# A decoder block with expert retrieval on one core: 24 instead of 16 tokens in rows, and the low parts of 22 weight tiles made beforehand

## The chip, the cores and the metric

The kernel runs on one NeuronCore of a Trainium2 chip. The metric is the device time of one execution in microseconds (us); the median of three runs is given. The engines are TensorE (PE; PEld is its weight load), VectorE (DVE), ScalarE (ACT), GpSimd (POOL) and SyncE (SP, which here only issues transfers). A name with q behind it (SPq, ACTq, POOLq) is an engine's instruction queue: issues of transfers, waits.

## The reference

One layer on x of 512 tokens by 1024 channels, in float32:

```
xn = rmsnorm(h, norm_mix_g)
h  = h + hybrid_mixer(xn, ...)      # gated short convolution + causal pooling, products with w_in,
                                    # w_conv_out, w_pool_out and w_out
xn = rmsnorm(h, norm_ffn_g)
h  = h + peer(xn, w_query, sub_keys, expert_u, expert_v)
return rmsnorm(h, norm_final_g)

def peer(...):                      # 8 heads, 128 x 128 = 16384 experts, 16 chosen per head
    q = xn @ w_query;  scores = q . sub_keys            # two halves of 128 keys per head
    v1, i1 = top_k(scores[0], 16);  v2, i2 = top_k(scores[1], 16)
    best, pos = top_k(v1[:, None] + v2[None, :], 16)
    e1 = i1[pos // 16];  e2 = i2[pos % 16];  experts = e1 * 128 + e2;  gates = softmax(best)
    a = gelu(xn . expert_u[experts]) * gates            # 128 experts per token
    return a @ expert_v[experts]
```

## The kernel before

Every matrix product is made of three float32r products (high x high, high x low, low x high) that sum in PSUM. A weight tile is 128 x 1024 float32 (512 KB). For each tile SP loads `w_raw`, ACT rounds it into `w_hi` (line 589), VectorE subtracts to get `w_lo` (L1157), and TensorE makes 8 blocks x 3 matmuls (`tile_product`, L922 to L924). There are four slots (`SLOTS`) for each; the loops run over groups of four tiles, b being the slot. Counting semaphores tie them: `hi_done`, `lo_done`, `job_done` (tiles whose products are done), `bank_free`. SP loads tile n when `lo_done` has passed tile n - 4; ACT rounds it when TensorE has done tile n - 4.

The stages in order: 32 tiles of `w_in` with convolution and pooling (`in_block`), 4 pool tiles, 32 gate tiles (sigmoids, `merged_hi`/`merged_lo`), 8 of `w_out`, 16 of `query` with the scores; then the experts.

The experts: tokens 0 to 127 (`GT`) are worked in rows: GpSimd gathers for each of their 128 pairs one row of `u_rows` per token (`gather`, L538, an indirect transfer of 128 rows of 4 KB into one of 4 `ROW_SLOTS`), and VectorE multiplies and sums (`dot`, L1522), later the same with `v` (`v_row`, L1711). The other 384 tokens (`DT`) are worked densely: U holds all 16384 experts in 128 tiles (`u_tile`, 32 steps of 4), ACT applies gelu (`gelu_tile`, L746) and stores the activation to `act_dram`, except for the last `KEPT_STEPS` steps, which stay in memory. Of the 384, the last `EXTRA` = 16 tokens are taken out of the dense U product, so that its columns are `DENSE`, 368 of them; their pairs are worked in rows too, in groups of 8 tokens by 16 (`lay_extra`, `turn_extra`, `dot_extra`), with their values carried into the gates (`extra_gates`, with three-part gates `masks_x`), and the activation there is one.

While TensorE runs `u_tile` steps 1 to 11 (`TOPK_STEPS` = 12), VectorE searches the top 16 (`search`, `decode`) with the splits of the tiles put between its parts, by hand (`splits`). `u_dots` puts the row dots in: one in every second search step, then lists (`DOTS_BEFORE`, `DOTS_ROUND`, `DOTS_PLAIN`). The first gathers wait for `experts_ready`. Steps 15 to 26 (`onehot_round`, 6 rounds of 2 steps) also build the dense gate matrix from one-hot masks made by VectorE (16 tokens a mask; L1082, two matmuls a token, three for `masks_x`), which ACT copies and stores to `g_dram`. After the U part the V part: 128 tiles, `mask_a` multiplies activation and gate, `v_tile` has 18 matmuls of 512 columns; VectorE works the rest of the u dots and all 128 v rows there.

In the first tiles the order is by hand as well: ACT rounds x blocks (`xg_hi`) in the order of their arrival, the two halves of weight tile 0 between them, and squares them for the norm.

Of the kernel before, what the change touches and what calls it, by code (L numbers as in the profile page):

```python
# [75 lines left out]
EXTRA = 16  # L76
SHARED = 8
EXTRA_GROUPS = EXTRA // SHARED
SPREAD = P // SHARED
# [3 lines left out]
ROW_SLOTS = 4  # L83

# [14 lines left out]
U_STEPS = KEYS // SLOTS  # L99
TOKENS_PER_GROUP = 4  # L100
# [7 lines left out]
DOTS_TOPK = 1  # L108
# [3 lines left out]
ROWS_V = (DOTS_TOPK * (TOPK_STEPS // 2 - 1) + sum(DOTS_BEFORE) + ROUNDS * sum(DOTS_ROUND)  # L112
          + (U_STEPS - 1 - PLAIN_AT) * sum(DOTS_PLAIN))
# [5 lines left out]
assert U_STEPS - KEPT_STEPS >= PLAIN_AT and KEPT_STEPS == 5  # L119
# [100 lines left out]
def build(nc, x_t, params_d, w_in_d, pool_d, gate_d, w_out_d, query_d, keys_d, u_d, v_d, u_rows, gain_d, out_d,  # L220
          act_dram, g_dram, index_dram, extra_dram):
    ctx = ExitStack()
    with ctx:
# [11 lines left out]
        scratch = fixed("scratch", [P, 2, T])  # L235
        row_stat = fixed("row_stat", [P, T])
# [27 lines left out]
        norm_sq = in_loop("norm_sq", [P, T])  # L264
        gate_loop = MemoryMap(nc, front.at)
# [38 lines left out]
        expert_last = small("expert_last", [P, PAIRS], U32)  # L304
# [3 lines left out]
        gate_x = small("gate_x", [P, EXTRA_PARTS, EXTRA], BF16)  # L308
        assert small.at <= nc.sbuf_usable_end and small.at >= max(rest.at, after_topk.at)
        beside_xn = MemoryMap(nc, xn_at)  # L310
        x_extra = [beside_xn(f"x_extra{h}", [P, NB, T])[:, :, 0:GT] for h in range(EXTRA_GROUPS)]
# [4 lines left out]
        in_scratch = MemoryMap(nc, scratch_at)  # L316
        e1_b = in_scratch("e1_b", [P, DT], F16)
        e2_b = in_scratch("e2_b", [P, DT], F16)
        gate_b = in_scratch("gate_b", [P, GATE_PARTS, DT], F16)
        assert in_scratch.at <= scratch_at + 4 * 2 * T  # L320

        masks = [region(f"masks{k}", [P, 1 + GATE_PARTS, MASKED // 2, KEYS, 2], F16)
                 for k, region in enumerate((g_build, MemoryMap(nc, masks_at)))]
        masks_x = MemoryMap(nc, masks_at)("masks_x", [P, 1 + EXTRA_PARTS, MASKED // 2, KEYS, 2], BF16)
# [15 lines left out]
        def kept_at(k, b):  # L340

            if k == 0:
                return act_in[:, b, :]
            if k == 1:
# [3 lines left out]
            if k < KEPT_STEPS - 1:  # L348
                return kept[:, k - 2, b, :]
# [1462 lines left out]
```

## Time and profile before

| | us |
|---|---|
| median of three runs | 1618.13 (1618.07 to 1619.25) |
| the profiled execution | 1618.06 |
| its span, first to last instruction | 1616.2 |
| TensorE busy | 1607.6 (99%) |
| VectorE busy | 1281.6 (79%) |
| ACT busy | 690.6 (43%) |
| GpSimd busy | 370.1 (23%) |

The profile is of one execution. Busy time is the time in which an engine ran at least one instruction; a line's duration is from an instruction's start to its end, and as matmuls overlap in TensorE's pipeline, durations are longer than the distance from one start to the next. The granted TensorE clock was 1.0 throughout, the higher of its two levels (2.4 GHz). GpSimd does nothing from 3.6 us until 548 us.

### The profile page before, as it was taken

To read this page: it belongs to the slowest core of one execution; us is meant where nothing else is said; L and a number is where in the kernel's file an instruction comes from. 1 tells how busy PE (TensorE), PEld (TensorE's weight loads), DVE (VectorE), ACT (ScalarE), POOL (GpSimd) and SP (SyncE) were. 2 spreads that over 40 slices of the span, in tenths; PEclk is the share of its full clock that TensorE was granted. 3 is DMA by queue.
4 is the path that set the end of the run, shared out by engine and by line. 5 is a ranking of instruction groups with operands and counts; after the bars stand their busy time and mean duration, and the time that the engine had idled before them with its cause. 6 is when DMAs were issued, how large, how long until landed. Compare 5 with 4: busy or idle time off the path is not lost.

```text
span 1616.2 us, 25174 instructions
## 1 busy us (share of the span) xinstructions
PE 1607.6 (99%) x8581; PEld 1422.9 (88%) x8581; DVE 1281.6 (79%) x2311; ACT 690.6 (43%) x921; POOL 370.1 (23%) x286
## 2 busy tenths in 40 slices
PE   9999999999999999999999999999999999999998
PEld 7888888888888999999999999998888888888887
DVE  6855733335457999998999998778898999998997
ACT  5323423333325433334666766433334333333333
POOL 0000000000000100003222222433453445554551
PEclk9999999999999999999999999999999999999999
DMA  4322332222321655658899999998999999999994
GB/s 170 131 93 97 116 109 91 94 100 94 115 81 64 224 185 194 212 191 334 318 367 364 377 359 374 403 376 324 387 413 367 402 414 398 403 415 393 414 378 161
DMA packets 126919, 424.34 MB, mean 263 GB/s; under 512 B 16384, under 2 KB 19472, under 8 KB 125200
## 3 DMA queue, kind: packets, MB, share of 16 engines
q1 hardware_dynamic: 75168, 232.85, 39.3%
q0 software_dynamic: 39264, 142.64, 23.0%
q10 hardware_dynamic: 12432, 48.26, 7.6%
q8 instruction: 18, 0.29, 0.1%
q14 instruction: 37, 0.30, 0.0%
HBM read 375.18 MB, written 48.51 MB: 262 GB/s over the span
## 4 chain that ended last, share of the span: by engine, by line
PE 99%; DMA 0%; DVE 0%; ACT 0%; SPq 0%; issue 0%; ACTq 0%
PE bank L922 21%; PE bank L923 20%; PE bank L924 20%; PE bank L1104 11%; PE bank L1106 11%; PE bank L1105 11%; PE bank L1082 3%; PE bank L988 1%; DMA w_raw<-w_in 0%; PE bank L968 0%; PE bank L967 0%; PE bank L969 0%; PE bank L1118 0%; DVE u_lo L1203 0%; PE bank L1039 0%; PE bank L940 0%
## 5 line engine op out<-in xcount | busy, mean ns | idle before, releaser
L1157 DVE TENSOR_TENSOR w_lo<-w_raw,w_hi 128x1024 fp32r<-128x1024 f32 x347 | 423.4, 1220 | 147.3 <-ACT w_hi L589 142.3
L589 ACT ACTIVATE w_hi<-w_raw 128x1024 fp32r<-128x1024 f32 x347 | 366.3, 1057 | 353.2 <-PE bank L1106 214.9
L922 PE MATMUL bank<-xn_hi,w_hi 128*128 128x368 f32 (+1 forms) x1472 | 516.6, 351 | 0.1
L924 PE MATMUL bank<-xn_hi,w_lo 128*128 128x368 f32 (+1 forms) x1472 | 510.7, 347 | 0.0
L923 PE MATMUL bank<-xn_lo,w_hi 128*128 128x368 f32 (+1 forms) x1472 | 510.6, 347 | 0.0
L538 POOL DMA_INDIRECT rows<-u_rows,expert x128 | 156.0, 1218 | 958.5 <-DVE expert L1558 544.4
L1104 PE MATMUL bank<-w_hi,a_hi 128*128 128x512 f32 x768 | 298.9, 389 | 0.0
L1106 PE MATMUL bank<-w_hi,a_lo 128*128 128x512 f32 x768 | 298.8, 389 | 0.0
L1105 PE MATMUL bank<-w_lo,a_hi 128*128 128x512 f32 x768 | 298.8, 389 | 0.0
L922 PEld LDWEIGHTS bank<-xn_hi,w_hi 128*128 128x128 f32 x1472 | 276.2, 188 | 17.8 <-issue 0.6
L924 PEld LDWEIGHTS bank<-xn_hi,w_lo 128*128 128x128 f32 x1472 | 276.1, 188 | 17.6
L923 PEld LDWEIGHTS bank<-xn_lo,w_hi 128*128 128x128 f32 x1472 | 276.4, 188 | 17.2 <-issue 0.2
L538 POOL DMA_INDIRECT rows<-v,expert x128 | 189.3, 1479 | 189.5 <-DVE out_tok L1711 172.8
L1106 PEld LDWEIGHTS bank<-w_hi,a_lo 128*128 128x128 f32 x768 | 144.1, 188 | 30.1
L1105 PEld LDWEIGHTS bank<-w_lo,a_hi 128*128 128x128 f32 x768 | 144.2, 188 | 29.9
L1104 PEld LDWEIGHTS bank<-w_hi,a_hi 128*128 128x128 f32 x768 | 144.1, 188 | 29.8
L1711 DVE SCALAR_TENSOR_TENSOR out_tok<-rows,dots,out_tok 128x1024 f32<-128x1024 f32 x128 | 163.8, 1280 | 8.0 <-DMA rows<-v,expert 4.6
L1522 DVE SCALAR_TENSOR_TENSOR rows<-rows,x_tok 128x1024 f32<-128x1024 f32 x128 | 154.7, 1218 | 18.2 <-DMA rows<-u_rows,expert 18.1
L746 ACT ACTIVATE act_out<-bank 128x368 f32<-128x368 f32 x112 | 53.6, 479 | 219.9 <-PE bank L924 209.8
L848 ACT ACTIVATE a_hi<-a_f 128x384 fp32r<-128x384 f32 x128 | 67.0, 523 | 99.6 <-DVE a_f L1692 96.9
L760 ACT ACTIVATE g_sb<-bank 128x512 f32<-128x512 f32 x96 | 101.3, 1172 | 4.8 <-PE bank L1082 4.8
L1698 DVE TENSOR_TENSOR a_lo<-a_f,a_hi 128x384 fp32r<-128x384 f32 x128 | 70.4, 550 | 0.0
(225 smaller groups left out, 1381.7 us busy)
## 6 DMA issues: line engine op xcount, KB each, us to landing
w_raw<-u SPq DMA_DIRECT2D x128, 512.0 KB
w_raw<-v SPq DMA_DIRECT2D x128, 512.0 KB
g_dram<-g_sb ACTq DMA_DIRECT2D x12, 2048.0 KB, 10.6
g_in<-g_dram SPq DMA_DIRECT2D x84, 256.0 KB
act_dram<-act_out ACTq DMA_DIRECT2D x54, 384.0 KB
act_in<-act_dram SPq DMA_DIRECT2D x54, 384.0 KB
w_raw<-gate SPq DMA_DIRECT2D x32, 512.0 KB
w_raw<-w_in SPq DMA_DIRECT2D x31, 512.0 KB
```

The lines of the kernel that those rows point to most:

```text
L538: pool.indirect_dma_start(out=rows[:, slot, :], out_offset=None, in_=table.rearrange("a p d -> (a p) d"), in_offset=bass.IndirectOffsetOnA ...
L589: act.activation(w_hi[:, slot, :], w_raw[:, slot, :], ACT.Copy).then_inc(hi_done, 1)
L760: act.activation(g_sb[:, k, :, t:t + TOKENS_PER_GROUP].rearrange("p e t -> p t e"), bank[4 + q % SLOTS][:].rearrange("p (t e) -> p t e", e ...
L922: pe.matmul(out, hi, x_hi, start=k == 0, stop=False)
L923: pe.matmul(out, hi, x_lo, start=False, stop=False)
L924: last = pe.matmul(out, lo, x_hi, start=False, stop=k == NB - 1)
L1104: pe.matmul(out, a_h, v_hi, start=False, stop=False)
L1105: pe.matmul(out, a_h, v_lo, start=False, stop=False)
L1106: return pe.matmul(out, a_l, v_hi, start=False, stop=final)
L1157: dve.tensor_tensor(w_lo[:, slot, :], w_raw[:, slot, :], w_hi[:, slot, :].bitcast(F32), ALU.subtract).then_inc(lo_done, 1)
L1522: dve.scalar_tensor_tensor(rows[:, slot, :], rows[:, slot, :], 1.0, x_tok[:], ALU.mult, ALU.mult, accum_out=dots[:, ds(r)]).then_inc(rows_ ...
L1711: dve.scalar_tensor_tensor(out_tok[:], rows[:, slot, :], dots[:, ds(r)], out_tok[:], ALU.mult, ALU.add).then_inc(v_rows_used, 1)
```

## The change

- `EXTRA` goes from 16 to 24: three groups of 8 tokens, a third `x_extra` in the memory of `scratch`, the dense product of 360 columns. Three-part gates now hold for the last 32 tokens (`EXTRA_SPAN`), in two masks. `extra_t` is fetched in six transfers of four tokens, one before each of six `gelu_tile` calls, in place of one transfer.
- The number of u dots goes from 144 to 152. In the search steps 2 to 11 there are two in each (20) where there was one in every second (5); the V part has 37 instead of 44.
- 22 low parts, those of the odd slots (b = 1, 3) of U steps 2 to 12, are no longer made by VectorE. After tile 3 GpSimd loads each such tile (`low_raw`), multiplies it by -1 into float32r (`low_part`), adds the tile to it by an accumulating transfer, and stores the sum to `low_dram`, in two slots. ACT waits for all the stores ahead of the gate loop, as the slots lie where the gate loop has its tiles. In the retrieval GpSimd loads each low part straight into `w_lo` when the tile four before is done, in program order with its gathers, and TensorE waits for it. VectorE's next split counts two on `lo_done`.
- Six steps are kept instead of five; the first kept one lies in `x_extra`.
- At the start ACT and VectorE work the second half of weight tile 0 after x block 3 instead of after block 1, and the first two squares after weight tile 1.

The core of the diff:

```diff
-EXTRA = 16
+EXTRA = 24
 SHARED = 8
 EXTRA_GROUPS = EXTRA // SHARED
+EXTRA_LOAD = 4
+EXTRA_BANK = (6, 4, 6)
...
-DOTS_TOPK = 1
+DOTS_TOPK = 2
...
-EXTRA_FIRST = DOTS_TOPK * (TOPK_STEPS // 2 - 1) + sum(DOTS_BEFORE)
+EXTRA_FIRST = DOTS_TOPK * (TOPK_STEPS - 2) + sum(DOTS_BEFORE)
 EXTRA_END = EXTRA_FIRST + EXTRA
 EXTRA_SHOWN = EXTRA_FIRST - sum(DOTS_BEFORE) + ROW_SLOTS
-assert EXTRA_END <= EXTRA_FIRST + 2 * sum(DOTS_ROUND) and EXTRA == MASKED
-KEPT_STEPS = 5
...
+KEPT_STEPS = 6
+assert U_STEPS - KEPT_STEPS >= PLAIN_AT - ROUND and KEPT_STEPS == 6
+KEPT_J = DT // P
...
+def low_tile(k):
+
+    return SLOTS * (k // 2 + 2) + 2 * (k % 2) + 1
...
+        low_raw = in_loop("low_raw", [P, LOW_SLOTS, D])
+        low_part = in_loop("low_part", [P, LOW_SLOTS, D], F32R)
...
                     if b % 2 == 1 and g >= KEPT_STEPS:
 
-                        sp.wait_ge(af_ready, b + 1 if g == KEPT_STEPS else SLOTS * (g - 1) + b + 1)
+                        sp.wait_ge(af_ready, SLOTS * (1 if g == KEPT_STEPS else g - 1) + b + 1)
...
+            def load_low(k):
+
+                slot, times = k % LOW_SLOTS, k // LOW_SLOTS
+                if times > 0:
+                    pool.wait_ge(low_stored[slot], 16 * times)
+                pool.dma_start(low_raw[:, slot, :], u_d[low_tile(k)]).then_inc(low_raw_loaded[slot], 16)
+
+            def sum_low(k):
+
+                slot, times = k % LOW_SLOTS, k // LOW_SLOTS
+                pool.wait_ge(low_raw_loaded[slot], 16 * (times + 1))
+                pool.tensor_scalar(low_part[:, slot, :], low_raw[:, slot, :], -1.0, None, ALU.mult
+                                   ).then_inc(minus_high, 1)
+                pool.wait_ge(minus_high, k + 1)
+                pool.dma_start(low_part[:, slot, :], u_d[low_tile(k)], accum_op=ALU.add).then_inc(low_summed[slot], 16)
+
+            def store_low(k):
+
+                slot, times = k % LOW_SLOTS, k // LOW_SLOTS
+                pool.wait_ge(low_summed[slot], 16 * (times + 1))
+                pool.dma_start(low_dram[k], low_part[:, slot, :]).then_inc(low_stored[slot], 16)
+
+            pool.wait_ge(job_done, SLOTS)
+            for k in range(N_LOW + 2):
+                if k >= 2:
+                    store_low(k - 2)
+                if 1 <= k <= N_LOW:
+                    sum_low(k - 1)
+                if k < N_LOW:
+                    load_low(k)
...
+            def load_low_part(k):
+
+                pool.wait_ge(job_done, AT_U + low_tile(k) - SLOTS + 1)
+                pool.dma_start(w_lo[:, low_tile(k) % SLOTS, :], low_dram[k]).then_inc(low_loaded[k % 2], 16)
+
             for q in range(U_ROWS):
+                if q >= ROW_SLOTS and (q - ROW_SLOTS) % DOTS_TOPK == 0:
+                    step = (q - ROW_SLOTS) // DOTS_TOPK + 3
+                    for n in range(1, 4) if q == ROW_SLOTS else (step,) if step < TOPK_STEPS else ():
+                        load_low_part(2 * n - 2)
+                        load_low_part(2 * n - 1)
...
-                if j == 1:
+                if j == NB // 2 - 1:
                     act.wait_ge(raw_loaded[0], 16)
                     act.activation(w_hi[:, 0, HALF:], w_raw[:, 0, HALF:], ACT.Copy).then_inc(hi_done, 1)
-                    square_x(0)
-                    square_x(1)
             split_weight(1, 1, 1)
-            for j in range(2, NB):
+            for j in range(NB):
...
+            for k in range(LOW_SLOTS):
+                act.wait_ge(low_stored[k], 16 * len(range(k, N_LOW, LOW_SLOTS)))
             with act.Fori(0, NB) as i:
...
+            def load_extra(k):
+
+                tokens = slice(EXTRA_LOAD * k, EXTRA_LOAD * (k + 1))
+                act.dma_start(extra_t[:, tokens], extra_dram[tokens, :].rearrange("t p -> p t"),
+                              allow_slow_non_contiguous=True).then_inc(extra_loaded, 16)
+
             def g_round(s, last=False):
                 for b in range(ROUND * SLOTS):
+                    if isinstance(s, int) and s == ROUNDS - 2 and b < EXTRA // EXTRA_LOAD:
+                        load_extra(b)
...
+                if whole is not None:
+                    pe.wait_ge(hi_done, n + 1)
+                    pe.wait_ge(*whole)
+                elif halves:
...
+            def u_tile(step, b, parts=None, low=False):
+                tile_product(SLOTS * step + (AT_U + b), b, step + (USES_U + 1), xn_hi, xn_lo, parts, NB, tokens=DENSE,
+                             whole=(low_loaded[b // 2], 16 * step - 16) if low and b % 2 == 1 else None)
...
+                u_tile(1, b)
+            with pe.Fori(2, TOPK_STEPS + 1) as step:
+                for b in range(SLOTS):
+                    u_tile(step, b, low=True)
+            with pe.Fori(TOPK_STEPS + 1, ONEHOT_AT - 1) as step:
...
-                        if last_round and q >= GROUPS_PER_ROUND - SLOTS:
-                            held, parts = masks_x, EXTRA_PARTS
+                        if last_round and q // SLOTS >= EXTRA_MASK % MASKS_PER_ROUND:
+                            held, parts = masks_x[q // 4 % 2], EXTRA_PARTS
...
+            def split_weight(n, slot, tiles=1):
 
                 dve.wait_ge(hi_done, n + 1)
                 dve.tensor_tensor(w_lo[:, slot, :], w_raw[:, slot, :], w_hi[:, slot, :].bitcast(F32),
-                                  ALU.subtract).then_inc(lo_done, 1)
+                                  ALU.subtract).then_inc(lo_done, tiles)
...
+                from_memory = lambda group, b: 2 <= group <= TOPK_STEPS and b % 2 == 1
+                if not from_memory(step + 1, b):
+                    last = from_memory(step + 1, b - 1) if b > 0 else from_memory(step, SLOTS - 1)
+                    split_weight(SLOTS * step + (AT_U + SLOTS + b), b, 2 if last else 1)
...
-                    u_dots(rows_done, DOTS_TOPK)
-                    rows_done += DOTS_TOPK
                 else:
                     search(chunk, i, at, [a, b, c, none])
                     decode(chunk, 2 * (i - 1), at[0], d)
+                if n >= 2:
+                    u_dots(rows_done, DOTS_TOPK)
+                    rows_done += DOTS_TOPK
```

## Rows read from the trace of the kernel before

**Rows 1.** The profile's page, part 4: the chain that ended last, by engine.

```profile
PE 99%; DMA 0%; DVE 0%; ACT 0%; SPq 0%; issue 0%; ACTq 0%
```

**Rows 2.** Timeline of TensorE, first and last of 46 starts, then of 62.

```profile
119.66 0.39 PE L924 MATMUL bank<-xn_hi,w_lo 128*128 128x512 f32 x1
...
129.86 0.39 PE L924 MATMUL bank<-xn_hi,w_lo 128*128 128x512 f32 x1
...
699.79 0.33 PE L922 MATMUL bank<-xn_hi,w_hi 128*128 128x368 f32 x1
...
709.95 0.33 PE L923 MATMUL bank<-xn_lo,w_hi 128*128 128x368 f32 x1
```

**Rows 3.** Busy time by stretch of the span, columns named in the text below.

```profile
40.00:187.00 147.00, 147.00 (x651) 121.70 (x650) 98.11 (x138) 45.64 (x60) 0.00 (x0) 1.00 0.31 106
...
546.00:755.00 209.00, 208.94 (x1254) 208.57 (x1253) 197.31 (x732) 77.91 (x110) 21.67 (x21) 1.00 0.65 221
755.00:1010.00 255.00, 255.00 (x2030) 248.22 (x2029) 237.34 (x270) 171.84 (x206) 70.60 (x58) 1.00 0.96 359
```

**Rows 4.** The chain that ended last in order of time: start us, length us, what.

```profile
755.45 0.98 PE bank L1061 x9
768.42 0.94 PE bank L1082 x16
...
997.67 1.39 PE bank L1082 x24
```

**Rows 5.** Timeline of the start, then the transfers issued in its first 20 us.

```profile
2.15 0.70 SPq L437 DMA_DIRECT2D h_t<-x_t  x1
...
10.90 2.55 ACT L604 ACTIVATE u_hi<-h_t,params 128x512 fp32r<-128x512 f32 x4
...
14.58 1.05 ACT L589 ACTIVATE w_hi<-w_raw 128x1024 fp32r<-128x1024 f32 x1
...
16.94 0.50 PE L922 MATMUL bank<-u_hi,w_hi 128*128 128x512 f32 x1
...
h_t<-x_t SPq DMA_DIRECT2D x1, 512.0 KB, 8.4
```

**Rows 6.** The page, part 5: groups of instructions, columns as the page names them.

```profile
L1157 DVE TENSOR_TENSOR w_lo<-w_raw,w_hi 128x1024 fp32r<-128x1024 f32 x347 | 423.4, 1220 | 147.3 <-ACT w_hi L589 142.3
...
L924 PEld LDWEIGHTS bank<-xn_hi,w_lo 128*128 128x128 f32 x1472 | 276.1, 188 | 17.6
...
L1522 DVE SCALAR_TENSOR_TENSOR rows<-rows,x_tok 128x1024 f32<-128x1024 f32 x128 | 154.7, 1218 | 18.2 <-DMA rows<-u_rows,expert 18.1
```

**Rows 7.** Timeline of TensorE at tile 4, of ACT before gate tile 4.

```profile
35.43 0.50 PE L922 MATMUL bank<-u_hi,w_hi 128*128 128x512 f32 x1
...
220.73 1.06 ACT L589 ACTIVATE w_hi<-w_raw 128x1024 fp32r<-128x1024 f32 x1 [4.38 <-PE bank L924]
```

**Rows 8.** Transfers with us to landing; groups of GpSimd's instructions.

```profile
out<-out_sb SPq DMA_DIRECT2D x7, 256.0 KB, 2.0
...
keys_t<-keys SPq DMA_DIRECT2D x1, 1024.0 KB, 5.5
...
index_dram<-expert_last POOLq DMA_DIRECT2D x1, 8.0 KB, 1.6
...
L553 POOL DMA_DIRECT2D expert_extra<-index_dram x2 | 1.2, 594 | 0.0
...
L533 POOL TENSOR_SCALAR_AFFINE_SELECT ident<-ident 128x128 f32<-128x128 f32 x1 | 0.3, 293 | 0.2 <-POOL iota_key L530 0.2
...
L525 POOL MEMSET z_pad<- 128x2 f32 x1 | 0.1, 96 | 0.0
```

**Rows 9.** Timeline of GpSimd and of ACT, then transfers from 546 to 570 us.

```profile
552.40 0.94 POOL L538 DMA_INDIRECT rows<-u_rows,expert  x1 [0.30 <-issue]
...
559.20 0.48 ACT L746 ACTIVATE act_out<-bank 128x368 f32<-128x368 f32 x1 [2.66 <-PE bank L924]
...
GB/s 273 0 0 0 266 379 106 232 369 321 314 328 239 341 382 389 335 259 253 300 294 376 411 410 415 403 246 41 20 164 321 348 343 343 10 0 0 0 0 0
```

More of the change, by code:

```diff
@@ L83 @@
 ROW_SLOTS = 4
+LOW_SLOTS = 2
 TOP_A, LOW_B = 4, 4
@@ L99 @@
 U_STEPS = KEYS // SLOTS
+N_LOW = 2 * (TOPK_STEPS - 1)
 TOKENS_PER_GROUP = 4
@@ L235, in build @@
         scratch = fixed("scratch", [P, 2, T])
+        row_stat_at = fixed.at
         row_stat = fixed("row_stat", [P, T])
@@ L307, in build @@
         extra_t = small("extra_t", [P, EXTRA])
-        gate_x = small("gate_x", [P, EXTRA_PARTS, EXTRA], BF16)
+        gate_x = small("gate_x", [P, EXTRA_PARTS, EXTRA_SPAN], BF16)
         assert small.at <= nc.sbuf_usable_end and small.at >= max(rest.at, after_topk.at)
         beside_xn = MemoryMap(nc, xn_at)
-        x_extra = [beside_xn(f"x_extra{h}", [P, NB, T])[:, :, 0:GT] for h in range(EXTRA_GROUPS)]
+        x_extra = [beside_xn(f"x_extra{h}", [P, NB, T])[:, :, 0:GT] for h in range(2)]
+        x_extra.append(MemoryMap(nc, scratch_at)("x_extra2", [P, NB, GT])[:])
         assert beside_xn.at <= scratch_at
@@ L366, in sem @@
             return ctx.enter_context(nc.semaphore(name))
+        low_raw_loaded = [sem(f"low_raw_loaded{k}") for k in range(LOW_SLOTS)]
+        minus_high = sem("minus_high")
+        low_summed = [sem(f"low_summed{k}") for k in range(LOW_SLOTS)]
+        low_stored = [sem(f"low_stored{k}") for k in range(LOW_SLOTS)]
+        low_loaded = [sem(f"low_loaded{k}") for k in range(SLOTS // 2)]
         x_loaded = [sem(f"x_loaded{k}") for k in range(X_PARTS)]
@@ L742, in gelu_tile @@
                     to = kept_at(step - (U_STEPS - KEPT_STEPS), b)
-                if not stored and step < U_STEPS - 1:
-                    act.activation(to[:, DU:], ones[:, 0:EXTRA], ACT.Copy).then_inc(ones_set, 1)
-                    act.wait_ge(ones_set, SLOTS * (step - (U_STEPS - KEPT_STEPS)) + b + 2)
-                act.activation(to[:, 0:DU], bank[b][:, DENSE], ACT.Gelu).then_inc(act_ready, 1)
+                if not stored and step == U_STEPS - KEPT_STEPS:
+                    whole = KEPT_J - 1
+                    act.activation(to[:, whole, DU - whole * P:], ones[:, 0:EXTRA], ACT.Copy).then_inc(ones_set, 1)
+                    act.activation(to[:, 0:whole, :], bank[b][:, GT:GT + whole * P].rearrange("p (j t) -> p j t", t=P),
+                                   ACT.Gelu).then_inc(ones_set, 1)
+                    act.wait_ge(ones_set, 2 * b + 3)
+                    act.activation(to[:, whole, 0:DU - whole * P], bank[b][:, GT + whole * P:T - EXTRA], ACT.Gelu
+                                   ).then_inc(act_ready, 1)
+                else:
+                    if not stored and step < U_STEPS - 1:
+                        act.activation(to[:, DU:], ones[:, 0:EXTRA], ACT.Copy).then_inc(ones_set, 1)
+                        act.wait_ge(ones_set, SLOTS * (step - (U_STEPS - KEPT_STEPS) + 1) + b + 2)
+                    act.activation(to[:, 0:DU], bank[b][:, DENSE], ACT.Gelu).then_inc(act_ready, 1)
                 split_weight(SLOTS * step + (AT_U + SLOTS + b), b, step + (AT_U // SLOTS + 2))
@@ L1047, in _ @@
                         pe.wait_ge(scores_ready, HALVES)
+                    elif b == 1:
+                        pe.wait_ge(x_tok_ready, 2)
                     else:
-                        pe.wait_ge(x_tok_ready, 2)
+                        pe.wait_ge(x_extra_ready, 2)
                     turn_extra(b)
-            with pe.Fori(1, ONEHOT_AT - 1) as step:
+            for b in range(SLOTS):
+                u_tile(1, b)
+            with pe.Fori(2, TOPK_STEPS + 1) as step:
+                for b in range(SLOTS):
+                    u_tile(step, b, low=True)
+            with pe.Fori(TOPK_STEPS + 1, ONEHOT_AT - 1) as step:
                 for b in range(SLOTS):
@@ L1212, in _ @@
                                       ALU.subtract).then_inc(lo_done, 1)
-                    dve.wait_ge(squared, 2)
-                    chain.did(dve.tensor_tensor(squares[:, 0, :], squares[:, 0, :], squares[:, 1, :], ALU.add))
             split_weight(1, 1)
-            for j in range(2, NB):
+            for j in range(1, NB):
                 dve.wait_ge(squared, j + 1)
-                chain.wait()
+                if j > 1:
+                    chain.wait()
                 add = dve.tensor_tensor(squares[:, 0, :], squares[:, 0, :], squares[:, j, :], ALU.add)
```

81 lines of the change are left out of this document (45 added, 36 removed).

## The prediction, made before the change was run

> **What bounds the kernel.** First the page: of the span of 1616.2 us the chain that ended last is 99% TensorE [rows 1]. So the time is the sum of TensorE's own work plus the gaps in it, and an edit counts only if it shortens a matmul, adds one, or makes TensorE wait. Next I ask whether a matmul's cost follows its columns. The PE timeline shows 46 starts of 512-column matmuls from 119.66 to 129.86 us, one every 10.20/45 = 0.2267 us, and 62 starts of 368-column ones from 699.79 to 709.95 us, one every 10.16/61 = 0.1666 us [rows 2]. (The duration printed, 0.33 or 0.39, holds the pipeline's depth and is no spacing.) The slope is 60.1 ns over 144 columns, 0.417 ns a column, and 13 ns are fixed. Last, the stages: how near VectorE and the transfers are to full where the change gives them work [rows 3]. Columns there: length, then busy us of PE, PEld, DVE, ACT, POOL, clock, DMA share, GB/s. VectorE is 67% busy in the input products, 94% in the retrieval (546 to 755 us), 93% in the one-hot rounds (755 to 1010 us), where the DMA share is 0.96. TensorE is full in all three.
>
> **The change part by part.**
> *24 tokens in rows.* The dense products of the retrieval run over 360 columns instead of 368: 128 tiles x 8 blocks x 3 products = 3072 matmuls, 8 x 0.417 = 3.34 ns each: -10.26 us. A tile of 24 products falls from 4.00 to 3.92 us.
> The third group of 8 tokens costs eight more transposes; nine took 0.98 us [rows 4], so +0.87 us. The gates come in three parts for the last 32 tokens instead of the last 16: 16 more 128-column matmuls. 16 took 0.94 us and 24 took 1.39 [rows 4]: 0.45 per eight, +0.90 us.
> *The start.* ACT now converts x blocks 2 and 3 before the second half of weight tile 0, and all squares after weight tile 1. Before, ACT came to block 2 only at 10.90 us; tile 1's weights were converted at 14.58 and its products began at 16.94 us [rows 5]. The x part issued on SP at 2.15 us lands 8.4 us later, at 10.6 us [rows 5]: now blocks 2 and 3 are done before it, blocks 4 to 7 take 2.6 us from 10.6, the weights 1.05 us more (14.3 us), their low part on VectorE 1.22: tile 1 begins at 15.6 us, 1.35 earlier. Tile 2 then waits for the squares' sum and its low part and begins some 1.05 us earlier. I take -1.05 us; bounds 0 and -1.6.
> *VectorE.* In the retrieval it loses 22 splits of 1.22 us (26.8) and gains 15 dots of 1.22 (18.3) [rows 6]: from 197 to 189 us in a stage that shrinks from 209 to 205. In the one-hot rounds its work stays (one mask part more, 1.2 us), and the stage gets 3 us shorter: 237.3 of 255 becomes 238.5 of 252, 95%. Behind the retrieval products it has 7 dots less. All this is off the path as long as it stays under 100%: no cost. Cover gone, a step costs the difference.
> *Kept step, loads in pieces.* Four activations fewer to store and to fetch, six small transfers in place of one; ACT is idle half the time. No cost.
> *Making the 22 low parts.* A chain on GpSimd: load the tile, negate it (rounded), add the tile by an accumulating transfer, store; two slots. ACT waits for all stores before the gate products, since the slots' memory becomes merged_lo and the sigmoids. It begins when tile 3 is done, 35.43 - 1.05 = 34.4 us [rows 7]. Behind ACT's wait stand sig_a, the next w_hi (1.05) and VectorE's w_lo (1.22), and TensorE needs these for gate tile 4 at 220.73 - 1.05 = 219.7 us [rows 7]; so the stores must be in by 219.7 - 0.60 - 1.05 - 1.22 = 216.8 us. No row has such a transfer, so I bound it. 256 KB landed in 2.0 us and 1 MB in 5.5 (stages with free transfers), so 512 KB of data are worth 2.33; 8 KB from GpSimd landed in 1.6 us [rows 8]: load and store 3.9 us each. The adding transfer: no less than 3.9; if the data part doubles because two sources are read, 6.2, and if everything doubles, 7.8. It moves three streams where a copy moves two, so I take 3.9 + 1.2 = 5.1. Issue on GpSimd: 0.6. Negation of 1024 elements: from 2 elements 0.096 us and 128 elements 0.293 [rows 8], 1.56 ns an element: 1.6 us. With two slots and GpSimd in program order a tile takes the larger of half the round, (3.9 + 1.6 + 5.1 + 3.9)/2 = 7.3, and 5.1 + 0.6 + 1.6 = 7.3 us. End: 34.4 + (3.9 + 1.6 + 5.1 + 3.9) + 21 x 7.3 = 202 us, 15 us in hand: no cost. It decides at 8.0 us a tile, that is an adding transfer of 5.8 us. Transfers there: 106 GB/s at a share of 0.31 now, plus 1.57 MB every 7.3 us = 215 GB/s: 321, below the 359 of the one-hot rounds.
> VectorE and GpSimd: VectorE is busy 98 of 147 us there [rows 3]. The Trainium skill ("SBUF — State Buffer", "Who interferes with whom") says that a VectorE instruction with two inputs in SBUF and a GpSimd one that reads SBUF lock each other out for a whole instruction. Nothing in this trace runs arithmetic on GpSimd beside VectorE, so no run here shows it yet; what it would do is the first rival.
> *Loading them.* Two loads a step. Each is issued when the tile four before is done and needed three tiles (11.8 us) later, against 0.6 + 3.9 us plus contention (the stage goes from 221 to some 315 GB/s with 22 loads and 15 gathers more): hidden, but for the first. Behind such a load's wait on GpSimd's queue stand the two gathers of that step, whose dots come a step later: hidden. The count of low parts done now moves for an odd tile with the even one behind it, so SP's reload of an odd slot waits one split longer (4 us of some 12 that it has), and behind it the next load. The third group's transposes wait for the copies of the first, made a tile before. The first four gathers, the last of them issued at 552.40 us, fill the transfers (300 to 415 GB/s) until 561.6 us (the GB/s line has 40 slices of 0.6 us from 546 us) [rows 9]. The low part of tile 9 is queued behind them on the same queue. Its 0.52 MB at 400 GB/s end at 562.9 us and land at some 563.2, less the 1.05 won at the start: 562.2 us. Tile 9's products began at 559.1 us (ACT took tile 8's result at 559.20) [rows 9], now at 559.1 - 1.05 + 0.87 - 9 x 0.08 = 558.2 us. TensorE waits +4.0 us, once; bounds 0 (if the gathers are through sooner) and 6 (if w_raw's stream takes half of the 400, and landing takes another us). Behind the wait every later product is queued; ACT and VectorE only get ahead.
>
> **Sum**, against the profiled run's own 1618.06 us (span 1616.2; the median is 1618.13, so nothing to convert): -10.26 - 1.05 + 0.87 + 0.90 + 4.0 = -5.5, thus 1612.5 us.
>
> **Rivals.**
> (a) *The chain of low parts is late*, the one that ends slower. Condition: over 8.0 us a tile. If each negation waits for one VectorE instruction of 1.22 us, a tile takes 8.5 and the end is 34.4 + 15.7 + 178.5 = 228.6 us, 11.8 late, TensorE idle before gate tile 4: 1624.3 us. If the adding transfer takes 7.8 us, a tile takes 10.0, the end is 262 and the time 1657. For it: the margin is 7% a tile, and two of its terms are in no row. Against: negation and copies are taken high, since the queues there are two thirds empty.
> (b) *No wait at tile 9*: the transfers reach 415 GB/s in single slices, and w_raw can be put off; 1608.5 us.
> (c) *The one-hot rounds do not get faster.* VectorE at 95% and transfers at 0.96 leave 12 us and little else; if one is the bound, the 70 tiles from 755 us on keep their 0.08 us each: 1612.5 + 5.6 = 1618.1. Against: VectorE's idle time is spread over every round.
> (d) *The columns do not count any more*: PEld is busy 208.6 of 209 us in the retrieval [rows 3], a load 188 ns [rows 6] where a matmul starts every 167. If the load were the floor, the 10.26 are lost: 1622.8. Against: at the 2.4 GHz granted (clock 1.00 in every row) 512 columns are 213.3 ns and 368 are 153.3, and both spacings lie 13.3 ns above that, so the columns set the pace at both; a floor would have to lie in the 3.3 ns below.
>
> **Chances.** Forecast 0.43; (a) 0.31, of which 0.02 late by under 2 us, 0.08 by 2 to 9, 0.21 by more; (b) 0.12; (c) 0.09; (d) 0.05. 0.2% is 3.2 us, about what a measurement of this kernel can tell from no change, so the borders are 1614.9 and 1621.4. Faster: 0.43 + 0.12 + 0.02 = 0.57; same: 0.09 + 0.08 = 0.17; slower: 0.21 + 0.05 = 0.26. The range goes from a us under (b) to (a)'s first price, 1607.5 to 1624.5, and leaves out only the late half of (a). The forecast's own is 1609 to 1615.
>
> **What would show it.** Spacing of the 360-column matmuls 163.3 ns (d: 166.6). Tile 1 at 15.6 us. GpSimd's last store before 217 us and no idle TensorE before gate tile 4 (a: idle there, ACT's sig_a released by a store). One wait of TensorE near 558 us, some 4 us, released by the transfer of a low part, and no others at later odd tiles. VectorE under 97% between 750 and 1005 us. I am wrong if the accumulating transfer is far from a copy, or if loads in the retrieval land later than 11 us.

## The result and the profile after

The changed kernel takes 1684.18 us (median of four runs, 1681.18 to 1687.09), the kernel before 1618.69 us on the same chip: a ratio of 1.0404 (95% interval 1.0390 to 1.0417). It is 4% slower, not 0.35% faster as forecast. The profiled execution has 1681.18 us and a span of 1679.4, 63.2 us more than before. The page shows at once where to look. First the slices of the span, then the chain that ended last, both from the changed kernel's page:

```profile
PE   9999921999999999999999999999999999999998
...
PEclk9999965999999999999999999999999999999999
```

```profile
PE 73%; DMA 11%; DVE 8%; POOL 4%; issue 2%; ACT 1%; SPq 0%; DVEq 0%; ACTq 0%; POOLq 0%
```

TensorE is empty in one place, a seventh of the way in, and the chain that was 99% TensorE [rows 1] now holds transfers and GpSimd. The list of waits (engine, tile and line, what it waited for: us in total, times, longest us) names the place, and the timeline of TensorE shows it:

```profile
ACT L741 <- DMA low_dram<-low_part: 82.0, 1, 82.0
...
PE bank L1007 <- DVE w_lo L1250: 67.8, 3, 66.8
PE bank L1007 <- DMA w_lo<-low_dram: 2.5, 1, 2.5
```

```profile
219.13 0.39 PE L1009 MATMUL bank<-mix_hi,w_lo 128*128 128x512 f32 x1
...
286.29 0.79 PE L1007 MATMUL bank<-xn_hi,w_hi 128*128 128x512 f32 x1 [66.77 <-DVE w_lo L1250]
...
291.57 0.47 PE L1007 MATMUL bank<-xn_hi,w_hi 128*128 128x512 f32 x1
```

The releaser printed is VectorE's split, but that took 1.2 us. Behind it stands ACT, which waited 82.0 us for the last store of a low part (the 22nd), with the activations for gate tile 4 in its queue. This is rival (a)'s place and its signature, at nearly six times its first price (66.8 us for 11.8). Why the last store came so late is read from the chain that ended last, in order of time (start us, length us, what), one of its rounds and the end:

```profile
220.10 2.78 POOL low_part L573
222.88 0.29 issue
223.17 0.60 POOL low_part L576
223.77 6.02 DMA low_raw<-u
...
273.30 5.27 DMA low_part<-u
278.57 0.29 issue
278.86 2.98 DMA low_dram<-low_part
```

A round is negation 2.8, a pause of 0.3, issue of the adding transfer 0.6, then the landing of the next tile's load, 6.0 us here: some 10 us. Over all 22 it is 11.0 us a tile ((270.2 - 39.8)/21, from the first line below; median, shortest and longest of a negation are in it as 2772, 2767 and 3084 ns). The transfers' medians from issue to landing follow it, 512 KB each:

```profile
L573 POOL TENSOR_SCALAR low_part<-low_raw x22: 2767/2772/3084, 39.8 to 270.2; 128x1024 fp32r<-128x1024 f32 x22
...
low_raw<-u POOLq DMA_DIRECT2D x22, 512.0 KB, 6.9
low_part<-u POOLq DMA_DIRECT2D x22, 512.0 KB, 5.4
low_dram<-low_part POOLq DMA_DIRECT2D x22, 512.0 KB, 3.5
w_lo<-low_dram POOLq DMA_DIRECT2D x22, 512.0 KB, 5.6
```

By stretch (columns as for [rows 3]): the first answers to its first row, then the idle stretch, then its other two.

```profile
40.00:187.00 147.00, 147.00 (x650) 121.78 (x649) 101.05 (x138) 45.69 (x60) 62.71 (x52) 1.00 0.81 239
...
220.00:286.00 66.00, 0.00 (x0) 0.00 (x0) 1.07 (x1) 3.93 (x5) 28.37 (x23) 0.53 0.52 141
...
546.00:755.00 209.00, 206.53 (x1248) 199.92 (x1247) 187.31 (x796) 86.98 (x125) 31.03 (x36) 1.00 0.69 236
755.00:1010.00 255.00, 254.16 (x1911) 248.95 (x1911) 242.26 (x374) 156.05 (x194) 76.64 (x66) 1.00 0.95 357
```

The last two stretches are shifted against the kernel's stages by the 67 us. Over the idle stretch the granted clock is 0.53 in the mean, so for nearly all of it TensorE has the lower of its two levels (1.2 GHz), and it comes back at that level: the 12 matmuls from 286.29 to 291.57 start 0.44 us apart instead of 0.227, 2.6 us lost.

**Columns.** The TensorE timeline, first and last of 62 starts of 360-column matmuls, in two places (the first answers to the second pair of [rows 2]):

```profile
605.72 0.33 PE L1008 MATMUL bank<-xn_lo,w_hi 128*128 128x360 f32 x1
...
615.75 0.33 PE L1009 MATMUL bank<-xn_hi,w_lo 128*128 128x360 f32 x1
...
699.29 0.32 PE L1008 MATMUL bank<-xn_lo,w_hi 128*128 128x360 f32 x1
...
709.05 0.32 PE L1009 MATMUL bank<-xn_hi,w_lo 128*128 128x360 f32 x1
```

10.03/61 = 164.4 ns, and 9.76/61 = 160.0 ns: two spacings of one matmul, neither the 163.3 forecast. The shorter one holds from tile 9's wait at 627.6 us to another wait at 764.7, for 839 of the 3072.

**The balance** of the span, after less before: +66.8 (idle before gate tile 4), +2.6 (clock behind it), +2.6 (one wait at tile 9, starts at 627.59 and 630.39), +1.0 (a wait at 764.7), -1.3 (start: tile 4 begins at 34.14 us, 35.43 before [rows 7]), +1.8 (transposes and masks), and the columns 839 x 6.7 ns + 2233 x 2.2 ns = -10.5: +63.0 of 63.2.

### The profile page after: what moved, and what is told of

Its sections match the earlier page's. It is cut to its first block, busy times and chain, and to the rows that moved or that the text cites. A ratio compares the mean times of both kernels' runs of the same rounds, so it can differ in the third digit from the quotient of the medians.

```text
span 1679.4 us, 25386 instructions
## 1 busy us (share of the span) xinstructions
PE 1601.5 (95%) x8605; PEld 1415.5 (84%) x8605; DVE 1275.5 (76%) x2307; ACT 691.9 (41%) x932; POOL 489.9 (29%) x405
## 4 chain that ended last, share of the span: by engine, by line
PE 73%; DMA 11%; DVE 8%; POOL 4%; issue 2%; ACT 1%; SPq 0%; DVEq 0%; ACTq 0%; POOLq 0%
PE bank L1007 13%; PE bank L1008 13%; PE bank L1009 13%; PE bank L1198 10%; PE bank L1199 10%; PE bank L1197 10%; DMA low_raw<-u 9%; POOL low_part L573 4%; PE bank L1175 3%; DVE rows L1617 1%; DMA low_part<-u 1%; POOL low_part L576 1%; DVE less L1520 1%; DVE w_lo L1250 1%; DVE top_i L1519 1%
## 5 line engine op out<-in xcount | busy, mean ns | idle before, releaser
L1007 PE MATMUL bank<-xn_hi,w_hi 128*128 128x360 f32 (+1 forms) x1472 | 514.3, 349 | 70.1 <-DVE w_lo L1250 67.6
L1250 DVE TENSOR_TENSOR w_lo<-w_raw,w_hi 128x1024 fp32r<-128x1024 f32 x325 | 399.5, 1229 | 223.7 <-ACT w_hi L656 214.6
L1008 PE MATMUL bank<-xn_lo,w_hi 128*128 128x360 f32 (+1 forms) x1472 | 508.8, 346 | 0.0
L1009 PE MATMUL bank<-xn_hi,w_lo 128*128 128x360 f32 (+1 forms) x1472 | 508.3, 345 | 0.0
L595 POOL DMA_INDIRECT rows<-v,expert x128 | 178.2, 1392 | 217.1 <-DVE out_tok L1815 197.1
L822 ACT ACTIVATE act_out<-bank 128x360 f32<-128x360 f32 x108 | 51.0, 472 | 171.6 <-PE bank L1009 164.3
```

The source lines that it names most:

```text
L595: pool.indirect_dma_start(out=rows[:, slot, :], out_offset=None, in_=table.rearrange("a p d -> (a p) d"), in_offset=bass.IndirectOffsetOnA ...
L1007: pe.matmul(out, hi, x_hi, start=k == 0, stop=False)
L1008: pe.matmul(out, hi, x_lo, start=False, stop=False)
L1009: last = pe.matmul(out, lo, x_hi, start=False, stop=k == NB - 1)
L1250: dve.tensor_tensor(w_lo[:, slot, :], w_raw[:, slot, :], w_hi[:, slot, :].bitcast(F32), ALU.subtract).then_inc(lo_done, tiles)
```

## The experiments

Ten kernels. Eight undo, resize or reorder a part of the changed kernel, and two measure TensorE alone. Of each edit the lines that matter are shown.

**1. No low parts by GpSimd (no_low_chain).** 24 tokens in rows stay; VectorE makes all low parts, and the dots of the retrieval are as before.

```
-                from_memory = lambda group, b: 2 <= group <= TOPK_STEPS and b % 2 == 1
+                from_memory = lambda group, b: False
-            for k in range(N_LOW + 2):
+            for k in range(0):
-DOTS_TOPK = 2
+DOTS_TOPK = 1
```

> Changed kernel without the chain of low parts and with the row dots where they were before (one in every second search step); 24 tokens in rows, the sixth kept step and the new order of the start stay. Theory A (the loss of 65 us is the chain alone; the rest of the prediction's sum holds): 1618.1 - 10.3 - 1.3 + 0.9 + 0.9 = 1608.3 us, no idle TensorE after 16 us, matmuls of 360 columns 163.3 ns apart. Rival B (part of the loss, or of the gain, hangs on VectorE with 8 dots more in the V part, or on the one-hot rounds that cannot go faster): 1612 us or more, with waits of TensorE after 560 us.

Measured: 1616.66 us (ten runs), before 1618.40; ratio 0.9990 (0.9980 to 0.9999). The 67 us are gone, so they belong to the low parts. But the gain is not the forecast's (rival B: over 1612 us, with waits after 560). TensorE's waits, and its timeline close to V's end:

```profile
PE bank L1005 <- DVE w_lo L1248: 2.0, 3, 1.3
PE bank L1195 <- DVE a_lo L1800: 1.9, 1, 1.9
```

```profile
1592.96 0.39 PE L1197 MATMUL bank<-w_hi,a_lo 128*128 128x512 f32 x1
1595.25 0.47 PE L1195 MATMUL bank<-w_hi,a_hi 128*128 128x512 f32 x1 [1.90 <-DVE a_lo L1800]
...
1598.33 0.63 PE L1197 MATMUL bank<-w_hi,a_lo 128*128 128x512 f32 x1
1598.75 0.60 PE L1195 MATMUL bank<-w_hi,a_hi 128*128 128x512 f32 x1
```

A wait of 2 us there also brought TensorE to its lower level: starts 0.43 us apart until 1599. VectorE has eight more dots than before and no room for them behind the retrieval. So the low parts are not an extra: they pay for the rows.

**2. Four slots, negation in place (four_slots).** The load is issued two tiles ahead; all 22 low parts.

```
-LOW_SLOTS = 2
+LOW_SLOTS = 4
+        low_part = MemoryMap(nc, in_loop.at - 4 * LOW_SLOTS * D)("low_part", [P, LOW_SLOTS, D], F32R)
-            for k in range(N_LOW + 2):
-                if k >= 2:
-                    store_low(k - 2)
-                if 1 <= k <= N_LOW:
-                    sum_low(k - 1)
+            for k in range(N_LOW + 3):
+                if 2 <= k <= N_LOW + 1:
+                    sum_low(k - 2)
                 if k < N_LOW:
                     load_low(k)
+                if k >= 3:
+                    store_low(k - 3)
```

> Chain of 22 low parts with four slots, negated in place, each load issued two tiles before its negation. Theory A1 (a tile took 10.6 us because a load could be issued only behind the add of the tile before, and had to land, 6.9 us, before the next negation of 2.8): now the tile takes what GpSimd itself needs, 6 to 7 us, the last store lands near 195 us, no wait of ACT, 1611.8 us (1608.3 + 2.6 at tile 9 + 0.9 near 764 us). Rival A2 (the transfers of that stage are full, share 0.81, and each simply takes as long as the engines give): the tile stays at 9 us or more, the last store lands after 235 us, TensorE idles 20 us or more, 1630 us or more.

Measured: 1624.05 us, four runs from 1616.16 (the profiled one) to 1628.72; ratio 1.0042 (1.0026 to 1.0059). In the profiled run a tile takes 7.5 us, the last store releases ACT at 214.05, and TensorE has no gap ahead of the gates. GpSimd's negations, the stretch from 40 to 187 us, and ACT's timeline:

```profile
L573 POOL TENSOR_SCALAR low_part<-low_raw x22: 2797/2806/3192, 40.5 to 197.7; 128x1024 fp32r<-128x1024 f32 x22
```

```profile
40.00:187.00 147.00, 147.00 (x649) 121.36 (x648) 110.12 (x137) 45.43 (x59) 93.26 (x76) 1.00 1.00 297
```

```profile
214.05 1.28 ACT L741 ACT_TABLE_LOAD   x1 [13.63 <-DMA low_dram<-low_part]
```

The time lies between the two theories. The transfers are full, a share of 1.00 at 297 GB/s, so 7.5 us a tile is about what they allow here, only 0.5 us under the forecast's deciding 8.0. ACT's release at 214.05 comes 2.7 us before the forecast's 216.8, but the true deadline is earlier (see below) and leaves 1.2 us. That the other three runs are 8 to 13 us longer fits a chain that is sometimes that much later; this is not shown, as only the fastest of the four has a trace.

**3. Without the adding transfer (no_add).** The low parts are then only minus the high parts, so the result is not the reference's. The store waits for the negation alone.

```
-                pool.dma_start(low_part[:, slot, :], u_d[low_tile(k)], accum_op=ALU.add).then_inc(low_summed[slot], 16)
-                pool.wait_ge(low_summed[slot], 16 * (times + 1))
+                pool.wait_ge(minus_high, k + 1)
```

> The adding transfer is left out (the negated tile is stored as it is, so the low parts are not the reference's). Theory A1: the load is no longer queued behind an add: it lands in 4 to 5 us instead of 6.9, a tile takes 2.8 + 0.3 + 0.6 + 4.5 = some 8 us, last store near 217 us, 1611 to 1616 us. Rival A2: landing stays over 6 us, a tile takes 9.5 or more, 1640 us or more.

Measured: 1629.94 us (one run), between the two theories. A tile still takes (220.2 - 39.4)/21 = 8.6 us, and TensorE waits 11.5 us ahead of the gates. The load lands in 5.4 us beside the store (6.4) issued with it. So the adding transfer costs 2.4 us a tile, but without it a tile is still over 8.0.

**4. Fourteen low parts (14_tiles).** U steps 2 to 8 load theirs; the later steps split on VectorE.

```
-N_LOW = 2 * (TOPK_STEPS - 1)
+LOW_STEPS = 8
+N_LOW = 2 * (LOW_STEPS - 1)
-                from_memory = lambda group, b: 2 <= group <= TOPK_STEPS and b % 2 == 1
+                from_memory = lambda group, b: 2 <= group <= LOW_STEPS and b % 2 == 1
```

> Only 14 low parts (U steps 2 to 8) are made beforehand, VectorE splits the other eight; 20 dots in the search steps stay. Theory A: at 10.6 us a tile the last store lands at about 34 + 15 + 13 x 10.6 = 187 to 200 us, before ACT asks: no wait, 1611.8 us; VectorE at 199 of 205 us in the retrieval is still enough. Rival B: VectorE is too late in the last search steps: 1614 us or more with waits of TensorE between 700 and 800 us.

Measured: 1620.11 us (ten runs), ratio 1.0011 (1.0002 to 1.0021). No wait ahead of the gates: fourteen fit at the slow pace. Now the retrieval has the waits (rival B):

```profile
PE bank L1008 <- DVE w_lo L1251: 3.1, 2, 1.9
PE bank L1008 <- DMA w_lo<-low_dram: 2.8, 1, 2.8
```

With 15 dots more there and 8 splits back, VectorE is too late twice, and the first loaded part is late as before; a stretch at half clock follows that wait.

**5. The order alone (load_first).** Two slots; load of tile k, then negation and adding transfer of k - 1, then store of k - 2. The wait for a slot's last store moves from the load to the negation.

```
-                if times > 0:
-                    pool.wait_ge(low_stored[slot], 16 * times)
                 pool.wait_ge(low_raw_loaded[slot], 16 * (times + 1))
+                if times > 0:
+                    pool.wait_ge(low_stored[slot], 16 * times)
...
+                if k < N_LOW:
+                    load_low(k)
+                if 1 <= k <= N_LOW:
+                    sum_low(k - 1)
                 if k >= 2:
                     store_low(k - 2)
-                if 1 <= k <= N_LOW:
-                    sum_low(k - 1)
-                if k < N_LOW:
-                    load_low(k)
```

> The changed kernel with its 22 low parts, its two slots and all its memory; only the order on GpSimd's queue differs: load of tile k, negation and adding transfer of tile k-1, store of tile k-2. Theory A (the load that is issued behind the adding transfer sets the 10.6 us a tile): what is left is the store: it lands 3.5 us after its issue as now or 7.0 as in four_slots, then negation 3.1, issues 1.2, 7.8 to 11.3 us a tile and with the landings between these about 8.5 us, so the last negation starts at about 218 us instead of 270, TensorE waits 10 to 20 us ahead of the gate tiles and not 67, and the time is 1625 to 1640 us. Theory B (the transfers' bandwidth sets it, whatever the order): 10 us a tile or more, a wait over 50 us, and the time stays above 1665 us.

Measured: 1680.08 us (one run); TensorE waits 63.0 us, a tile takes (265.8 - 39.0)/21 = 10.8 us. GpSimd's queue, waits and landings:

```profile
105.24 2.77 POOL L573 TENSOR_SCALAR low_part<-low_raw 128x1024 fp32r<-128x1024 f32 x1 [5.79 <-DMA low_dram<-low_part]
108.31 0.93 POOL L576 DMA_DIRECT2D low_part<-u  x1 [0.30 <-POOL low_part L573]
108.91 0.91 POOL L582 DMA_DIRECT2D low_dram<-low_part  x1
109.45 0.90 POOL L565 DMA_DIRECT2D low_raw<-u  x1
115.22 2.77 POOL L573 TENSOR_SCALAR low_part<-low_raw 128x1024 fp32r<-128x1024 f32 x1 [4.87 <-DMA low_dram<-low_part]
...
low_dram<-low_part POOLq DMA_DIRECT2D x22, 512.0 KB, 6.4
```

The time is theory B's, its reason is not: this kernel moves no more bytes a tile than four_slots, which does it in 7.5 us. The load is out of the round, and the store has taken its place, now landing 6.4 us after its issue. My theory that the order alone was at fault falls. In both orders with two slots some transfer stands in the round beside the negation, and three transfers issued within 1.2 us land in 5.5 to 8.0 us each (medians). What four_slots has and this kernel has not is depth: four slots, and the load two tiles ahead. Four slots in the changed kernel's own order were not run, so how the two share the gain is not shown.

**6. All 15 dots early, no low parts by GpSimd (dots_early).** The first two edits of no_low_chain, without its third:

```
 DOTS_TOPK = 2
```

> 24 tokens in rows and 15 dots moved into the retrieval as in the changed kernel, but no low parts made by GpSimd: VectorE makes all of them itself. Theory A (VectorE has no room for both): its work in the retrieval passes TensorE's by some 10 us, TensorE waits for its low parts there for 8 to 15 us, the end of V is not late, and the time is 1622 to 1630 us. Theory B (VectorE has room as it is): no waits over 3 us, and the time is 1610 to 1614 us.

Measured: 1629.53 us (one run), theory A. TensorE waits 12.4 us in the retrieval, four times, up to 4.1, for VectorE's splits, and its clock drops behind three of the four. Beside it four_slots_20 (below) has the same dots and loads its low parts: 16 us less.

**7. Four slots and 20 low parts (four_slots_20).** The chain of four_slots; U step 2 splits for itself, so no loaded part is queued behind the first four gathers.

```
-N_LOW = 2 * (TOPK_STEPS - 1)
+N_LOW = 2 * (TOPK_STEPS - 2)
-                from_memory = lambda group, b: 2 <= group <= TOPK_STEPS and b % 2 == 1
+                from_memory = lambda group, b: 3 <= group <= TOPK_STEPS and b % 2 == 1
```

> As four_slots, with 20 low parts instead of 22: the first step after the gate tiles makes its own. Theory A (nothing but the chain's fit stands in the way of the columns' gain): no wait before the gate tiles, the wait for a loaded low part at U step 2 and its half-clock stretch (2.8 and 1.7 us in four_slots) gone, so 1616.2 - 4.5 = 1611.7 us, range 1609 to 1614. Theory B (the transfers and GpSimd's negations beside VectorE cost as much as they save, wherever they are): VectorE is late elsewhere in the retrieval, and the time stays at 1615 to 1620 us.

Measured: 1613.37 us (seven runs, 1612.55 to 1614.96), before 1618.41; ratio 0.9972 (0.9960 to 0.9983). Theory A; it beats both kernels. TensorE's waits in full, and the stretch from 40 to 187 us:

```profile
PE bank L1029 <- POOL p_pad L552: 1.0, 1, 1.0
PE bank L1007 <- DVE u_lo L1296: 0.9, 1, 0.9
PE bank L1007 <- DVE w_lo L1250: 0.7, 2, 0.4
```

```profile
40.00:187.00 147.00, 147.00 (x650) 121.74 (x649) 108.67 (x137) 45.76 (x60) 91.74 (x75) 1.00 1.00 292
```

Two low parts fewer (7.8 us a tile here, 20 of them) end the chain a good 10 us earlier than in four_slots (last negation 186.8), and the scatter of 12.6 us there is down to 2.4.

**8. The dots in the plain steps (dots_in_plain).** As no_low_chain, and:

```
-DOTS_PLAIN = (2, 2, 1, 2)
+DOTS_PLAIN = (2, 2, 2, 3)
```

> 24 tokens in rows, no low parts by GpSimd, and the eight more dots put into the rounds' plain steps instead of V's end. Theory A (in no_low_chain the end of V was late because VectorE had eight dots more there, 1.9 us of wait and a stretch at half clock): both go, and the time is 1616.7 - 4 = about 1612.7 us, range 1611 to 1615. Theory B (the plain steps have no room either): the rounds get longer by about what V gets shorter, and the time stays within 1 us of 1616.7.

Measured: 1629.78 us (four runs), ratio 1.0073 (1.0056 to 1.0090). This is 13 us more than in no_low_chain, where theory B had at most 1: TensorE waits eight times between 1044 and 1098 us, 0.4 to 2.6 us each. There is no room for eight dots there either.

**9. Matmul spacing by width (spacing).** Nothing of the reference is computed: TensorE alone, the kernel's three products, 13 widths, then 360 columns again after eight pauses.

> Nothing of the reference is computed: TensorE alone multiplies, 13 widths from 512 down to 256 columns, 8 tiles of 24 matmuls each, and then 360 columns again after 8 pauses of growing length. Theory A, of the prediction: one spacing for each width, a line through 166.7 ns at 368 columns and 226.7 at 512, so 163.3 at 360. Theory B, from the changed kernel: at 360 columns there are two spacings, about 160 and 164.4 ns, and which of them holds changes at a pause; then some other widths that are no multiple of 16 should show two as well, and 368 and 352 only one. Theory C: the two spacings come from what VectorE or the transfers do beside it; then only one is seen here.

From the timeline, 144 starts of each width:

```
columns  512   384   376   368   364   360   356   352   344   336   320   288   256
ns       226.7 173.3 173.3 166.7 166.7 164.4 160.0 161.1 153.3 153.3 146.7 131.7 120.0
360 columns again, once without a pause and behind eight pauses of growing length: seven times 164.4, then 160.0, 160.0
```

For 360 columns in the last run, first and last of 61 starts:

```profile
705.11 0.32 PE L69 MATMUL bank<-x_lo,w_hi 128*128 128x360 f32 x1
...
714.71 0.32 PE L69 MATMUL bank<-x_lo,w_hi 128*128 128x360 f32 x1
```

Between multiples of 16 the steps are not even: 376 takes the time of 384 and 364 that of 368, but 344 that of 336, and 356 takes 160.0, less than 352. Theory A is out, since 360 columns have two spacings, and so is C: VectorE did nothing here, and the transfers moved 1 GB/s. The line of the forecast is met at 384, 368, 336, 320 and 256 columns and missed by 1 to 3 ns at the others. Theory B's two spacings at other widths were not put to the test, since each of these ran only once, with no pause.

**10. What changes the spacing (between).** TensorE alone again: 39 blocks of 48 matmuls of 360 columns, one matmul of another width between two, no pause.

> Nothing of the reference is computed: TensorE alone does 39 blocks of 48 matmuls of 360 columns, and between two blocks one matmul of another width, 8 to 512 columns, with no pause. Theory A (which of the two spacings of 360 columns holds is a matter of phase that any odd matmul may shift): several blocks have 160 ns and the others 164.4, changing after certain widths. Theory B (only an idle TensorE changes it): all 39 blocks have 164.4 ns.

The first block began at the lower clock, behind an idle TensorE, and has 160.0 ns once the clock is up; the second, which a single matmul of 360 columns joins to it, has 160.0 as well. Behind the first matmul of 8 columns it is 164.4 or 164.6, except for six blocks with 160.0: behind single matmuls of 104, 128, 192, 328 and 344 columns and behind the third of 352. So no idle time is needed: theory A. The same width, 352, was followed once by 160.0 and twice by 164.4, so the width alone does not decide it. What does stays open.

## Why the prediction was wrong

**What bounds the kernel**: right. TensorE sets the time, and every microsecond of the loss is a gap in it or a stretch at its lower clock.

**Making the 22 low parts, "no cost"**: this step failed; it cost 66.8 + 2.6 us. The forecast had 7.3 us a tile and 15 us in hand; the tile took 11.0. The wait on ACT was placed rightly. The deadline was 1.5 us too late, because ACT loads the sigmoid's table first: before the change it did so ahead of time, now it does so behind the wait (first line before, second after):

```profile
201.20 1.28 ACT L674 ACT_TABLE_LOAD   x1
...
282.06 1.28 ACT L741 ACT_TABLE_LOAD   x1 [82.04 <-DMA low_dram<-low_part]
```

From ACT's release to TensorE's start it is 286.29 - 282.06 = 4.2 us, the forecast had 2.9; gate tile 4 was due at 286.29 - 66.77 = 219.5, so the stores at 215.3, and a tile could take 7.9 us instead of 8.0. The terms of the tile are what failed:
- The negation was 1.6 us, extended from rows of 2 and 128 elements that are two other operations (and 0.096 + 1022 x 1.56 ns is 1.7); it took 2.77, 2.7 ns an element. The Trainium skill (GPSIMD Engine Reference, "Elementwise — side-by-side cycle accounting") gives about 1.8 cycles of 1.2 GHz an element in the best case, which makes an estimate of 1.5 us for this one. The trace's 2.77 is nearly twice this best case.
- Load and store were 3.9 us each, taken from transfers that met nobody: the load took 6.9, the store 3.5 (6.4 or more in the four kernels in which something was issued with it). The adding transfer was 5.1 and took 5.4, so here the term I thought uncertain was the right one (with full transfers, in four_slots, it took 7.0).
- By the forecast's own formula these terms give (6.9 + 2.8 + 5.4 + 3.5)/2 = 9.3 us, already over 8.0, and 5.4 + 0.6 + 2.8 = 8.8. The program order adds the rest: the load is issued behind the adding transfer of the tile before it and the next negation waits for its landing, 2.8 + 0.3 + 0.6 + 6.9 = 10.6. The rest up to 11.0 is in one early round, in which the chain goes through an adding transfer of 8.1 us and a store of 5.8. The forecast had no such round among its two. So what failed is the pace of a tile: two terms of it mis-sized (negation and load), and the longest round left out.
- "321 GB/s, below the 359 of the one-hot rounds" compared unlike streams: with this chain the share was 1.00 at 297 GB/s already (four_slots, 7.5 us a tile).

**VectorE beside GpSimd**: rival (a) had GpSimd wait for VectorE. The traces show nearly the reverse: 19 of the 22 negations take 2.77 or 2.78 us, with VectorE idle (after 220 us) and at work, and the longest 3.08, while VectorE's busy time for the same instructions goes from 98.1 to 101.1 us of 147 with 13 negations, and to 110.1 with 19 in four_slots. VectorE is held up only at a negation's start. Two pairs from the timeline of the changed kernel:

```profile
99.50 2.77 POOL L573 TENSOR_SCALAR low_part<-low_raw 128x1024 fp32r<-128x1024 f32 x1 [2.73 <-DMA low_raw<-u]
100.89 1.23 DVE L1250 TENSOR_TENSOR w_lo<-w_raw,w_hi 128x1024 fp32r<-128x1024 f32 x1 [0.32 <-ACT w_hi L656]
...
165.86 2.77 POOL L573 TENSOR_SCALAR low_part<-low_raw 128x1024 fp32r<-128x1024 f32 x1 [0.70 <-DMA low_raw<-u]
166.17 1.80 DVE L1250 TENSOR_TENSOR w_lo<-w_raw,w_hi 128x1024 fp32r<-128x1024 f32 x1 [0.32 <-ACT w_hi L656]
```

The four splits that begin within 0.8 us of a negation's start all end 2.11 us after that start, 1.38 to 2.03 us long; those that begin 1.0 us or more behind it take their usual 1.22, with the negation still running. `u_f<-bank,conv`, one of whose two inputs is in PSUM, takes 0.69 us with a negation beside it or without. By the Trainium skill ("SBUF — State Buffer", "Who interferes with whom") the two lock each other out where VectorE has two inputs in SBUF. The trace agrees as to which instructions are held up, but not that it is for a whole instruction, as the prediction has it: it is some 0.9 of 2.77 us. It cost TensorE nothing in this stage.

**24 tokens in rows**: right in sum, wrong in its term. 3.34 ns a matmul was read off a line through two widths; 360 columns give 2.2 ns or 6.7. The forecast's -10.26 came out as -10.5 in this run only because tile 9's wait happened to be followed by the shorter spacing; with 164.4 throughout, as in four_slots_20, it is -6.8. Rival (d) is out: 160 ns runs under a weight load of 188.

**Start**: -1.05 forecast, -1.3 measured, tile 1 at 15.51 (15.6). **Transposes and masks**: 24 gate matmuls still take 1.39 us and 16 take 0.94; the 24 more of TensorE's are all there (8605 for 8581), and nothing off shows.

**Loading**: one wait at tile 9, 2.6 us for 4.0, released by the low part's transfer, none at later odd tiles; the loads land in 5.6 us. Rival (b) is out. Not in the sum: in five of the other kernels a wait of 1.9 to 2.8 us is followed by some 3.4 us at TensorE's lower level, 1.7 us more; the changed kernel's own wait of 2.5 us is not.

**One-hot rounds**: rival (c) is out: in four_slots_20 nothing waits there, VectorE is busy 241.5 of 255 us (95%, as forecast), and the whole gain of the columns arrives. The span is 5.5 us less than before; columns, start, transposes with masks and two short waits in the retrieval give -6.8 - 1.5 + 1.8 + 0.6 = -5.9.

Once the low parts are in time, the change gives about the forecast's 1612.5 us (1613.4 in four_slots_20, which makes 20 of them), but part of that is luck: the columns gave 3.5 us less than forecast, and the wait of 4.0 us at tile 9 is not there, since that tile makes its own low part. The chance given to the low parts being late by more than 9 us was 0.21.

## What to carry to other kernels

A chain of transfers with two slots goes at the pace of its program order: write down, for each wait on the queue, which transfer was issued last before it, and add its landing beside the others; a landing read where a queue is empty is a lower bound, and here it was 3.9 against 6.9. When the margin is 0.7 us of 8.0 (9%; the forecast's 7% is a slip) and two terms are extrapolated, the extrapolated ones go to their upper ends first. A chain that everything hangs on should have depth (with four slots and the load two tiles ahead the 67 us of idle time are gone in the profiled run, 60 us in the median) and one or two items fewer than fit. Before cutting columns, measure the spacing at that very width.

## What was not expected of the hardware

- A 360-column matmul has two spacings, 160.0 and 164.4 ns, each stable for hundreds of matmuls; which one holds changed at waits and at single matmuls of another width, and what decides it is open. In this kernel the choice is worth 3072 x 4.4 = 13.5 us. 376 columns take the time of 384, and 344 that of 336.
- The chain's transfers use more of the engines than their bytes say: the stretch from 40 to 187 us went from 106 GB/s at a share of 0.31 [rows 3] to 297 at 1.00 in four_slots, that is 277 GB/s for each unit of share added, against 342 before. The adding transfer is only a part of it: without it (no_add, 226 GB/s at 0.70) it is still 308. As an estimate from these shares and the time a tile takes, the two plain transfers take 0.39 x 8.6 = 3.4 us of all engines, 1.7 each, and the adding one 1.8 (0.69 x 7.5 - 3.4) to 2.1 us (0.50 x 11.0 - 3.4).
- In the changed kernel a negation on GpSimd holds up VectorE's splits, which have both inputs in SBUF, only in its first 0.9 us of 2.77.
- Behind an idle stretch of 66.8 us TensorE ran at half its rate for 5.3 us, and behind some short waits for some 3.4 us. The length of the wait does not tell which: 1.9 us in no_low_chain and 2.8 in 14_tiles did it, 2.5 in the changed kernel and 2.4 in dots_early did not, and with TensorE alone (spacing) 1.8 and 2.1 us did, 2.5 and 2.8 did not.
